# Mamba core: D times x on TensorE, exponentials of the sums spread by DMA, products with C on VectorE

## The reference, cut to what matters

```python
a_cs = jnp.cumsum(a, axis=-1)                    # sums of dt * A along the tokens
decay_in = jnp.exp(segsum(a))                    # exp of differences of the sums
cb = jnp.einsum('bclgn,bcsgn->bgcls', cc, bc)    # C . B, one per group
y_diag = jnp.einsum('bgcls,bgrcls,bcsgrp->bclgrp', cb, decay_in, x)
y_off = jnp.einsum('bclgn,bcgrpn,bgrcl->bclgrp', cc, prev_states, jnp.exp(a_cs))
...
y = y + d_skip * xs                              # D times x
y = y * jax.nn.silu(z)                           # then an RMS norm per group and the output product
```

## Time and profile before

| | |
|---|---|
| time, median of 3 runs | 2170.89 us (2166.93 to 2173.28) |
| the profiled execution | 2171.69 us, span 2169.9 us |
| mean granted TensorE clock | 0.964 of full speed |
| TensorE busy | 2010.6 us, 93% of the span |
| VectorE busy | 1323.8 us, 61% |
| ScalarE busy | 688.0 us, 32% |
| GpSimd busy | 200.8 us, 9% |
| loads of `afb` | 32 of 256 KB, 3.2 us from issue to landing |

### The profile page before, as it was taken

The page is one execution under the profiler, slowest core; times in us unless marked ns, Lnnn a source line. Parts: engine busy times, 40 slices in busy tenths (PEclk is TensorE's granted clock), DMA queues, the critical chain, the costliest instruction groups (busy, mean ns, idle before and its releaser), DMA issues. The chain is left out here.

```text
span 2169.9 us, 24946 instructions
## 1 busy us (share of the span) xinstructions
PE 2010.6 (93%) x10136; PEld 1680.3 (77%) x10136; DVE 1323.8 (61%) x1844; ACT 688.0 (32%) x913; POOL 200.8 (9%) x140
## 2 busy tenths in 40 slices
PE   5899999999988889999999999999899797698998
PEld 2688888878776768888887888888787784398997
DVE  6565546687765566554676555476764648845544
ACT  3422222232200232222223222222444435634442
POOL 1000001100032310000110000011000003340001
PEclk9999999999989989999999999999999899989999
DMA  8454436544500134443554444264433422444554
GB/s 318 151 168 148 142 92 188 164 146 155 190 5 1 59 116 155 155 136 105 181 171 141 160 136 155 77 205 154 148 116 94 129 84 73 121 128 160 180 155 137
DMA packets 274446, 298.25 MB, mean 137 GB/s; under 512 B 8896, under 2 KB 249120, under 8 KB 272416
## 3 DMA queue, kind: packets, MB, share of 16 engines
q1 hardware_dynamic: 270640, 285.44, 41.2%
q10 hardware_dynamic: 3696, 11.27, 1.4%
HBM read 290.31 MB, written 6.37 MB: 137 GB/s over the span
## 5 line engine op out<-in xcount | busy, mean ns | idle before, releaser
L1465 PE MATMUL banks<-xh,wh 128*128 128x512 f32 (+1 forms) x2120 | 783.9, 370 | 46.5 <-DVE wl L872 21.3
L1466 PE MATMUL banks<-xl,wh 128*128 128x512 f32 (+1 forms) x2120 | 778.3, 367 | 0.0
L1467 PE MATMUL banks<-xh,wl 128*128 128x512 f32 (+1 forms) x2120 | 777.3, 367 | 0.0
L872 DVE TENSOR_TENSOR wl<-raw,wh 128x2048 fp32r<-128x2048 f32 (+1 forms) x196 | 405.3, 2069 | 336.4 <-ACT wh L551 335.0
L551 ACT ACTIVATE wh<-raw 128x2048 fp32r<-128x2048 f32 (+1 forms) x202 | 351.5, 1740 | 612.7 <-PE banks L1467 518.1
L1465 PEld LDWEIGHTS banks<-xh,wh 128*128 128x128 f32 x2120 | 409.6, 193 | 117.2 <-DVE wl L872 24.0
L1467 PEld LDWEIGHTS banks<-xh,wl 128*128 128x128 f32 x2120 | 408.8, 193 | 63.2
L1466 PEld LDWEIGHTS banks<-xl,wh 128*128 128x128 f32 x2120 | 409.5, 193 | 61.9
L1465 PE MATMUL banks<-gh,wh 128*128 128x512 f32 (+1 forms) x704 | 255.9, 364 | 5.1 <-DVE wl L872 4.0
L1466 PE MATMUL banks<-gl,wh 128*128 128x512 f32 (+1 forms) x704 | 255.3, 363 | 0.0
L1467 PE MATMUL banks<-gh,wl 128*128 128x512 f32 (+1 forms) x704 | 255.2, 363 | 0.0
(11 more groups left out here) (209 smaller groups left out, 1742.6 us busy)
## 6 DMA issues: line engine op xcount, KB each, us to landing
raw<-in_ffn_in SPq DMA_DIRECT2D x88, 1024.0 KB, 5.1
raw<-in_ffn_out SPq DMA_DIRECT2D x64, 704.0 KB, 4.9
ada_rawf<-in_ada_rest SPq DMA_DIRECT2D x60, 512.0 KB, 4.0
ada_rawo<-in_ada_rest SPq DMA_DIRECT2D x48, 512.0 KB, 4.1
raw<-in_mb_in_w SPq DMA_DIRECT2D x24, 1024.0 KB, 5.5
raw<-in_hy_in_w SPq DMA_DIRECT2D x12, 1024.0 KB, 5.2
afb<-decays SPq DMA_DIRECT2D x32, 256.0 KB, 3.2
raw<-in_mb_out_w SPq DMA_DIRECT2D x8, 1024.0 KB, 5.8
```

What stands on the lines that cost most here:

```text
L872: dve.tensor_tensor(wl[n_slot][:, 0:cols], raw[r_slot][:, 0:cols], wh[n_slot][:, 0:cols].bitcast(F32), ALU.subtract).then_inc(w_lo, 1)
L1465: pe.matmul(dst, h, x_hi, start=start, stop=False)
L1466: pe.matmul(dst, h, x_lo, start=False, stop=False)
L1467: return pe.matmul(dst, l_, x_hi, start=False, stop=stop)
```

## The change

D times x leaves `gate_y`: ScalarE multiplies x by D in place (after x has been turned for the scan), and TensorE adds it to the group's PSUM tile through the identity, as the first matmul of each pair. The exponentials of the sums are no longer made 128 partitions wide by ScalarE: ScalarE makes them once on the 64 rows of `dts`, writes them to the scratch tensor behind the sums, and SP loads them broadcast into `csx[r]`, each behind the load of `afb[r]` and behind a wait (`cs_used`) until TensorE has used the tile in the group before. The products with C are done by VectorE (`state_c`, one instruction a head, behind `exponents`), and GpSimd does nothing in the core.

```diff
@@ SP
-            sp.wait_ge(af_st, 32)
+            sp.wait_ge(af_st, 64)
             for g in range(GROUPS):
                 for r in range(HPG):
                     if g:
                         sp.wait_ge(d_done, g * HPG + r - 3)
                         sp.wait_ge(e_done, g * HPG + r - 3)
-                    sp.dma_start(afb[r][:], afscr[g * HPG + r].partition_broadcast(P)).then_inc(afb_in[r], 16)
+                    sp.dma_start(afb[r][:], afscr[0, g * HPG + r].partition_broadcast(P)).then_inc(afb_in[r], 16)
+                    if g:
+                        sp.wait_ge(cs_used, 2 * g - 1 + r // 2)
+                    elif r == 0:
+                        sp.wait_ge(dt_v, 4)
+                    sp.dma_start(csx[r][:].rearrange("p (a n) -> p a n", a=2),
+                                 afscr[1, g * HPG + r].partition_broadcast(P)).then_inc(cs_in[r], 16)
@@ ScalarE
             for d in range(2):
-                act.dma_start(afscr[:, d, :], dts[64 + 32 * d:96 + 32 * d, 5, :]).then_inc(af_st, 16)
+                act.dma_start(afscr[0, :, d, :], dts[64 + 32 * d:96 + 32 * d, 5, :]).then_inc(af_st, 16)
+            act.activation(dts[64:128, 6, :], dts[64:128, 5, :], ACT.Exp).then_inc(dt_e, 1)
+            act.wait_ge(dt_e, 4)
+            for d in range(2):
+                act.dma_start(afscr[1, :, d, :], dts[64 + 32 * d:96 + 32 * d, 6, :]).then_inc(af_st, 16)
...
+            def d_x(g):
+
+                for m in (2 * g, 2 * g + 1):
+                    act.activation(xb[:, 0, m, :], xb[:, 0, m, :], ACT.Copy, scale=dcol[:, m:m + 1]).then_inc(dx_done, 1)
+
+            act.wait_ge(tr_mm, 16)
+            d_x(0)
             for h in range(HEADS):
                 g, r = h // HPG, h % HPG
                 d_ = dm[h % 2]
+                if r == 1 and g + 1 < GROUPS:
+                    d_x(g + 1)
                 act.wait_ge(afb_in[r], 16 * g + 16)
-                if g:
-                    act.wait_ge(head_mm, h - 3)
-                act.activation(csx[r][:], afb[r][:].rearrange("p a n -> p (a n)"), ACT.Exp).then_inc(ex_done, 1)
                 if g:
                     act.wait_ge(m_done, h - 3)
@@ VectorE
+            def state_c(h):
+
+                g, r = h // HPG, h % HPG
+                dve.wait_ge(cs_in[r], 16 * g + 16)
+                cs = csx[r][:].rearrange("p (d n) -> p d n", d=2)
+                dve.tensor_tensor(cs, cs, csb[:, g, :].unsqueeze(1).to_broadcast([P, 2, L]), ALU.mult).then_inc(cs_done, 1)
+
             def gate_y(g):
...
-                for mt in range(2):
-                    m = g * 2 + (mt - 2)
-                    own.mark(dve.scalar_tensor_tensor(tt[3][:, mt * L:mt * L + L], xb[:, 0, m, :], dcol[:, m:m + 1],
-                                                      bank[4 + (g - 1) % 2][:, mt * L:mt * L + L], ALU.mult, ALU.add))
-                own.sync()
                 zz = zsb[:, g * 2 - 2:g * 2, :]
-                dve.tensor_tensor(zz, zz, tt[3][:].rearrange("p (a n) -> p a n", a=2), ALU.mult).then_inc(y_done, 1)
+                dve.tensor_tensor(zz, zz, bank[4 + (g - 1) % 2][:].rearrange("p (a n) -> p a n", a=2),
+                                  ALU.mult).then_inc(y_done, 1)
...
             token_major(8, 2)
+            state_c(0)
+            state_c(1)
             b_dot_c(0)
             for h in range(HEADS):
                 products(h)
                 if h + 2 < HEADS:
                     exponents(h + 2)
+                    state_c(h + 2)
@@ GpSimd
-            for h in range(HEADS):
-                g, r = h // HPG, h % HPG
-                pool.wait_ge(ex_done, h + 1)
-                cs = csx[r][:].rearrange("p (d n) -> p d n", d=2)
-                pool.tensor_tensor(cs, cs, csb[:, g, :].unsqueeze(1).to_broadcast([P, 2, L]), ALU.mult).then_inc(cs_done, 1)
@@ TensorE
+                    m = 2 * g + p
+                    pe.wait_ge(dx_done, m + 1)
+                    pe.matmul(bank[4 + g % 2][:, p * L:p * L + L], ident, xb[:, 0, m, :], start=True, stop=False)
                     pe.wait_ge(cs_done, g * HPG + 2 * p + 2)
                     for d in range(2):
                         for r, hc, y in pair:
-                            pe.matmul(y, ssb[:, d, hc], csx[r][:, d * L:d * L + L], start=d == 0, stop=False)
+                            ins = pe.matmul(y, ssb[:, d, hc], csx[r][:, d * L:d * L + L], start=False, stop=False)
+                    ins.then_inc(cs_used, 1)
                     pe.wait_ge(m_done, g * HPG + 2 * p + 2)
```

More of the change, by code:

```diff
@@ L370, in build @@
         e_done = sem("e_done")
-        ex_done = sem("ex_done")
+        cs_in = [sem(f"cs_in{r}") for r in range(HPG)]
+        cs_used = sem("cs_used")
+        dx_done = sem("dx_done")
         cs_done = sem("cs_done")
@@ L1937 @@
     kscr = nc.dram_tensor("filter_spectra", (P, 4, 5, 512), F32, kind="Internal").ap()
-    afscr = nc.dram_tensor("decays", (HEADS, 2, L), F32, kind="Internal").ap()
+    afscr = nc.dram_tensor("decays", (2, HEADS, 2, L), F32, kind="Internal").ap()
     cscr = nc.dram_tensor("silu_c", (2, D), F32, kind="Internal").ap()
```

## The result

The changed kernel takes 2174.0 us (median of 20 runs, 2171.46 to 2176.59), the kernel before, run beside it, 2170.65 us (median of 20). The ratio is 1.0014, 95% interval 1.0008 to 1.0021: 3.35 us more, real but within the 0.3% that I counted as no change. The forecast was 2175 us, + 4.0.

What follows compares the result with a forecast made beforehand. VectorE's list and an equally long three-engine loop bound the Mamba core at 9.8 us a group. Forecast 2170.9 + 4.0 (1.3 + 0.6 + 1.1 + 1.9 - 0.9) = 2174.9, rounded to 2175 us; 8-in-10 range 2169 to 2181.

Steps and rivals of the forecast that it cites:

- The hindrance: In each four-head group, GpSimd's products slow VectorE's two-SBUF-input instructions; removing them saves 1.45 us a group.
- the list: VectorE's back-to-back instructions in one group of four heads, a bound on the period: 9.86 us forecast, against 9.80 before.
- The products at 0.60 each: Four products with C a group, moved to VectorE, step 0.60 us each and add 2.40 us to its work.
- D times x: Per group, two TensorE matmuls of 0.53 us each; ScalarE's scaling copies hidden, at zero cost.
- The ring of three engines: Group loop through VectorE, TensorE's sum of squares, ScalarE's square and last exponential, back to VectorE: 10.12 us.
- The transfer's loop: Exponentials' DMA waits for TensorE to finish with the tile, then lands 3.3 us after issue: 10.2 us a group.
- P3: VectorE's products instruction of a group's fourth head (head 3), forecast to start 6.00 us after the second head's.
- P1: VectorE's products instruction of a group's second head (head 1); its recurrence marks the group's period, forecast 10.2 us.
- the late rival: Doubled traffic makes the exponentials' transfer land in 4.2 us: loop 11.1 us, total 2180.6 us, chance 0.2.
- The start: At the core's start, ScalarE's extra exponential, two DMA issues and a wait delay the copy of B: + 1.3 us.
- The end: The last gate, on the path to the next stage, loses its pair: - 0.9 us; output-weight loads cost nothing.
- TensorE's clock: The half-clock dip near 1830 us could cost up to 1.5 us; taken as nothing, kept for the range.

Runs made afterwards that it cites:

- e6: Kernel before with GpSimd's products with C left out (output not the reference's): ratio to before 0.9971, period 9.39 us.
- e2: Kernel before with only D times x moved to TensorE (ScalarE scales x) and squares in two tiles: 2159.65 us, ratio to before 0.9942.
- e8: Kernel before with D times x by TensorE through sixteen diagonal matrices made once, and squares in two tiles: ratio to before 0.9951.
- e7: Changed kernel with squares in two tiles, two sets of tiles for the exponentials, and products with C kept on GpSimd: 2164.68 us, ratio to before 0.9975.
- e5: Changed kernel with squares in two tiles and two sets of tiles for the exponentials of the sums: 2170.43 us, ratio to before 0.9999.
- e1: Kernel before with only D times x moved to TensorE (ScalarE scales x), exponentials and products with C as before: ratio to before 1.0001.
- e4: Changed kernel with two sets of tiles for the exponentials of the sums: ratio to before 1.0011, period 10.13 us.
- e9: Changed kernel with squares and exponentials each double-buffered, and ScalarE's copies of B ahead of the new exponential, its store and the mask's load: ratio to before 0.9984.
- e12: Kernel before with D times x on TensorE, squares in two tiles, and ScalarE's copies of B ahead of its three DMA issues: 2156.71 us, ratio 0.9942.

## Why the prediction was right

**The hindrance (- 1.45 a group): held.** Its removal is seen in the changed kernel and, with nothing else changed, in e6. The Trainium skill, GPSIMD Engine Reference, Specifications, says that GpSimd shares its SBUF interfaces with VectorE, in contention with instructions that have two SBUF inputs; the rows agree (0.344 against 0.636 us with two SBUF inputs, 0.675 undisturbed with one in PSUM). What I treated as a constant of the group is not one: it was 1.45 before, 0.9 in e2, 1.2 in e8, 1.8 in e7 (9.23 a group in the mean of six, less the 7.46 of the list).

**The products at 0.60 each: held.** e5 has the list as the only bound and takes 9.82, against the 9.86 of the sum. The strict reading of the Trainium skill, VectorE: DVE Perf Modes, section on the DRAIN, would have given 10.2; the same section adds that a next operation that nothing holds starts earlier, and by the rows these did (0.60 us apart).

**D times x: held.** The D matmuls step 0.63 us each in the steady groups (1856.96 to 1857.59), 0.1 more than taken, and ScalarE's copies 0.80 a pair. They cost nothing here because the wide exponentials are gone; e1 shows what they cost when these stay.

**The ring of three engines, 10.12: held** to 0.01 (e4).

**The transfer's loop, 10.2: the size held, the place only in part, and the two loops are nearly one.** I priced the load of head 2 at 3.3 us (3.1 to 3.4 in the steady groups) and let head 3's follow by 1.3 us, just in time. It followed by 2.4: 768 KB behind one release take longer than the spacing of the old burst. So in the changed kernel the wait stands mostly at head 3 (0.1 to 0.4 us, in four of the last five groups), and only once at head 2 (0.2 us, behind a landing of 3.4). Those at head 3 cost next to nothing: P3 comes 6.0 us behind P1 in these groups with the transfer (6.01 to 6.10) and without it (e4, 6.01 to 6.04), because ScalarE's exponential for P3 is no earlier. The mean period of 10.20 is the ring's 10.13 and 0.07 for the transfer. The forecast took the longer of two loops that lie 0.1 apart, and it would have been as good with the other. This is the late rival in a mild form: landings did rise to 4.1 to 4.7 us in the median, but not that of head 2's load, the first in its burst. The estimate of 2.6 us by the Trainium skill, DMA: Bandwidth & Descriptors, section Anatomy of one DMA, which is stated for another issuing path, isn't borne out by any load here: the least landing was 3.1 in the changed kernel and 3.0 before.

**The start (+ 1.3): held**, 1.26, and e9 and e12 show that it is the order on ScalarE and no more.

**The end (- 0.9): wrong.** The gate's pair is gone there too, but the last load of the exponentials lands 5.6 us after issue, and the first 1 MB of output weights (1024 KB) stands behind it in the same queue, issued 0.8 us later. By my reading the two share the DMA's engines. It costs 1.03 us of wait, P1 to P3 takes 5.54 against 4.93 us, and ScalarE's last square waits 0.25 us more for the sum of squares. I had argued only that the weights would be in time, and not what they do to the load ahead of them; that the weights are the cause is argued from the order and wasn't tested. For it: head 3's load landed in 4.6 to 4.8 us in the six groups before. Against it: a load of head 1 took 5.6 us as well (issued 1853.42), with no weights in the queue.

**TensorE's clock (nothing, up to 1.5): held.** The granted clock was 1.00 from 1812 on in the changed kernel, the dip at 1830 did not come back: the profile has 3.37 us of matmul in 1824 to 1828, against 1.77 before.

The stage grew by 4.70 us in the profile, 0.7 over the forecast, and nearly all of that is the end. The median grew by 3.35, which is 0.65 under the forecast; that both errors are small is in part luck, since the rest behind the stage varies between 277 and 280 us from profile to profile in kernels that do not differ there, more than the gap between the two figures.

## What to carry to other kernels

Before work is moved off the busiest engine, look for the second loop of the same length: here a spare tile for the squares was worth nothing in the changed kernel, and D times x on TensorE nothing in the kernel before, while the two together took 0.5 to 0.6% off the kernel before. (The spare tile alone in the kernel before was not run; that it is worth nothing there too is argued from VectorE's list without idle time.) A neighbour that blocks an engine through shared memory access is not a fixed cost but one of phase, so get its price with both lists in their final order. A DMA that replaces computed data brings its landing time into the loop of the buffer's reuse: give it a second buffer, and mind that loads released by one event land one behind the other.

## What the runs showed of the hardware

- In the kernel before, 256 KB broadcast loads landed in 3.0 to 3.6 us (median 3.1, 1825 to 1875). In the changed kernel (1822 to 1875), where four are issued within 1.4 to 2.1 us, the first of four landed in 3.1 to 4.1 us, the third in 4.6 to 5.6 and the fourth in 4.7 to 5.7. The core's DMA traffic was 216 GB/s at a mean busy share of 0.72 in the steady stretch (1843 to 1866), and 103 GB/s at 0.32 before.
- A blocked VectorE instruction ends about 0.15 us after GpSimd's does, and both instructions of the exponents can be hit (0.636 and 0.507 us in the mean in e7).
- TensorE's half clock (1.2 of 2.4 GHz) fell on different parts of group 0 from kernel to kernel, and the group with the same instructions took 8.66 us in e12 (granted clock 1.00 from 1810 on) and 10.11 in e2 (0.50 until 1814), with P0 at 1808.3 in both and TensorE busy for 2.9 and 3.0 us of 1804 to 1808. It took 9.22 us in e5 (0.50 from 1810 to 1814 and 0.57 to 1816, ahead of P1) and 10.44 in e9 (0.98 from 1810 to 1812 and 0.50 to 1814, behind P1). Why it lies where it does stays open.
